# Delta rule: a substitution by rows for the 16x16 diagonal blocks of the inverses

## What is computed

```python
decay = jnp.exp(jnp.where(tri, g[..., :, None] - g[..., None, :], -jnp.inf))
kk = jnp.einsum("bnhcd,bnhsd->bnhcs", k, k)
lower = jnp.where(strict, beta[..., :, None] * kk * decay, 0.0)
rhs = jnp.concatenate([v * beta[..., None], k * (beta * jnp.exp(g))[..., None]], axis=-1)
sol = lax.linalg.triangular_solve(lower, rhs, left_side=True, lower=True, unit_diagonal=True)
```

## Time and profile before

| | before |
|---|---|
| median of 3 runs | 1775.28 us (1773.97 to 1776.09) |
| the profiled execution, its own time | 1773.64 us |
| span of the profile | 1771.5 us |
| granted TensorE clock, mean | 0.988 |
| TensorE matmul busy | 1679.3 us (95% of the span) |
| VectorE, ScalarE, GpSimd busy | 875.3, 783.6, 201.5 us |

### The profile page before, as it was taken

The page is one execution under the profiler, slowest core; times in us unless marked ns, Lnnn a source line. Parts: engine busy times, 40 slices in busy tenths (PEclk is TensorE's granted clock), DMA queues, the critical chain, the costliest instruction groups (busy, mean ns, idle before and its releaser), DMA issues.

```text
span 1771.5 us, 21811 instructions
## 1 busy us (share of the span) xinstructions
PE 1679.3 (95%) x8436; PEld 1334.6 (75%) x8436; DVE 875.3 (49%) x1388; ACT 783.6 (44%) x1345; POOL 201.5 (11%) x233
## 2 busy tenths in 40 slices
PE   6899999999988899999999799999997999999998
PEld 4678888888877687677777588777675888888867
DVE  4746556556554535455555543544336532344346
ACT  3533543543543424565665622555544432243243
POOL 0111211111102200023232300000002000000011
PEclk9899999999999999999999999999998999999999
DMA  4111111111110322322222122211121333233321
GB/s 167 60 36 36 60 48 37 60 49 36 60 37 24 111 96 84 114 78 72 78 70 69 36 96 95 68 50 58 48 72 48 107 100 100 90 103 101 102 72 48
DMA packets 40165, 127.29 MB, mean 72 GB/s; under 512 B 4576, under 2 KB 9104, under 8 KB 40064
## 3 DMA queue, kind: packets, MB, share of 16 engines
q1 hardware_dynamic: 38112, 121.65, 20.8%
q0 software_dynamic: 1040, 3.27, 0.5%
q10 hardware_dynamic: 912, 0.99, 0.2%
HBM read 122.69 MB, written 2.15 MB: 70 GB/s over the span
## 4 chain that ended last, share of the span: by engine, by line
PE 83%; DVE 7%; ACT 6%; issue 3%; POOL 1%; DMA 0%; SPq 0%; ACTq 0%; DVEq 0%
PE ps L637 81%; ACT L L1521 3%; DVE wl L1713 2%; DVE L L2162 1%; PE ps L975 1%; PE ps L783 1%; DVE qkv L1749 1%; POOL h L2409 1%; ACT wh L1126 1%; DVE qb L1800 0%; ACT L L1473 0%; DMA wraw<-in_wa 0%; DVE mo L2285 0%; ACT xr L1390 0%; DVE U L2026 0%
## 5 line engine op out<-in xcount | busy, mean ns | idle before, releaser
L637 PE MATMUL ps<-xr,wh 128*128 128x512 f32 x2752 | 906.9, 411 | 15.5 <-DVE wl L1713 14.1
L637 PEld LDWEIGHTS ps<-xr,wh 128*128 128x128 f32 x2752 | 502.7, 190 | 139.6 <-issue 36.5
L637 PE MATMUL ps<-xr,wl 128*128 128x512 f32 x1376 | 542.1, 394 | 0.0
L1713 DVE TENSOR_TENSOR wl<-wraw,wh 128x1024 fp32r<-128x1024 f32 x214 | 261.3, 1235 | 153.3 <-ACT wh L1126 151.8
L637 PEld LDWEIGHTS ps<-xr,wl 128*128 128x128 f32 x1376 | 260.4, 189 | 57.3
L1126 ACT ACTIVATE wh<-wraw 128x1024 fp32r<-128x1024 f32 x214 | 220.3, 1047 | 20.3 <-PE ps L637 17.8
L637 PE MATMUL ps<-xm,wh 128*128 128x512 f32 x640 | 200.8, 395 | 12.8 <-DVE xm L2278 8.6
L637 PEld LDWEIGHTS ps<-xm,wh 128*128 128x128 f32 x640 | 120.2, 189 | 44.2 <-issue 9.8
L637 PE MATMUL ps<-xm,wl 128*128 128x512 f32 x320 | 125.3, 392 | 0.0
L2394 POOL TENSOR_SCALAR L<-L,m 128x256 f32<-128x256 f32 (+1 forms) x128 | 75.6, 611 | 325.5 <-DVE m L2177 325.5
L2338 POOL TENSOR_TENSOR Mm<-AT,masks 128x512 f32<-128x512 f32 x56 | 82.8, 1485 | 239.3 <-PE ps L637 122.8
(11 more groups left out here) (240 smaller groups left out, 1946.5 us busy)
## 6 DMA issues: line engine op xcount, KB each, us to landing
wraw<-in_wa SPq DMA_DIRECT2D x48, 512.0 KB, 3.3
wraw<-in_wb SPq DMA_DIRECT2D x32, 512.0 KB, 3.3
wraw<-in_wu SPq DMA_DIRECT2D x32, 512.0 KB, 3.3
wraw<-in_wd SPq DMA_DIRECT2D x32, 512.0 KB, 3.3
wraw<-in_wao SPq DMA_DIRECT2D x16, 512.0 KB, 3.4
wraw<-in_wbo SPq DMA_DIRECT2D x16, 512.0 KB, 3.3
wraw<-in_wc SPq DMA_DIRECT2D x16, 512.0 KB, 3.3
bias<-rel_rows SPq DMA_DIRECT2D x16, 256.0 KB, 3.7
```

Source lines behind the costliest of these rows:

```text
L637: return e.matmul(out, w, x, start=start, stop=stop, skip_group_check=True)
L1713: e.tensor_tensor(m.wl[:, i % N_SPLIT, :], m.raw[:, i % N_RAW, :], m.wh[:, i % N_SPLIT, :].bitcast(F), ALU.subtract).then_inc(s.wlo, 1)
```

## The change

The four lowest levels (blocks up to 16x16) are no longer made by products. GpSimd masks A to the 16x16 diagonal blocks in one multiplication (`m16`, a mask summed once at the start). VectorE adds the blocks of a row up into a compact 128x64 tile `dc` (each partition holds the 16 entries of its block's row, for 4 chunks), and 15 shuffles, one for each row r, copy row r of each block to all 16 partitions of that block (`nb`). GpSimd starts from the unit matrix and, for each r, does a product and a sum on up to 4x15 elements of `uc`; each of the 31 instructions waits for the one before. VectorE spreads `uc` into `U` (`U3`) and transposes it in blocks of 32x32 (`T3`). Three levels of products remain (4, 5 and 6). The transposed factor is made from `U` each time: on VectorE for level 5, by TensorE for level 6. `prep` keeps its 28 steps; 16 calls on TensorE are left.

```diff
 # TensorE, prep: calls 8 to 15
-        o = begin(8)
-        e.wait_ge(s.prep_v, prep_v(h, "U0"))
-        end(8, turn4(o, lambda n: U[:, n, :]), (s.prep_a, prep_a(h, "T")))
-        yield
-        call = 9
-        for i in range(1, 7):
+        yield from idle(6)
+        call = 8
+        for i in range(4, 7):
...
-            if i < 6:
-                o = begin(call)
-                e.wait_ge(s.prep_a, prep_a(h, f"P{i}"))
-                e.wait_ge(s.prep_v, prep_v(h, f"U{i - 1}"))
-                end(call, four(o, lambda n: U[:, n, :], lambda n: m.Pm[:, n, :]), (s.prep_v, prep_v(h, f"T{i}")))
-                call += 1
...
+            if i == 5:
+                o = begin(call)
+                e.wait_ge(s.prep_v, prep_v(h, "U5"))
+                end(call, turn4(o, lambda n: U[:, n, :]), (s.prep_a, prep_a(h, "T5")))
+                call += 1
+                yield
 # VectorE, prep
+        e.wait_ge(s.prep_o, prep_o(h, "D"))
+        did(e.tensor_reduce(m.dc[:], m.Mm[:, 1].rearrange("p n (b c) -> p n c b", b=8), AX.X, ALU.add, negate=True))
         o = product(5)
...
-        e.wait_ge(s.prep_o, prep_o(h, "M0"))
-        did(e.tensor_tensor(U, m.ident.unsqueeze(1).to_broadcast([128, 4, 128]), m.Mm[:, 0], ALU.subtract))
-        yield
-        yield from idle(3)
+        yield
+        after("dc")
+        if h:
+            e.wait_ge(s.inv, N_INV * h)
+        for r in range(15):
+            e.stream_shuffle(m.nb[:, r], m.dc[:].rearrange("p n c -> p (n c)"), [r] * 16 + [16 + r] * 16).then_inc(s.rows16, 1)
+        yield
+        yield from idle(6)
+        e.wait_ge(s.inv, N_INV * (h + 1))
...
+        did(e.tensor_tensor(U.rearrange("p n (b c) -> p n b c", b=8), m.uc[:].unsqueeze(2).to_broadcast([128, 4, 8, 16]),
+                            m.m16.rearrange("p (b c) -> p b c", b=8).unsqueeze(1).to_broadcast([128, 4, 8, 16]),
+                            ALU.mult))
+        after("U3")
...
+        did(e.transpose(m.Tm[:].rearrange("p n c -> p (n c)"), U.rearrange("p n c -> p (n c)")))
+        yield
+        for call, i in ((9, 4), (11, 5), (14, 6)):
+            yield
             o = product(call)
             after(f"U{i - 1}")
             did(e.tensor_tensor(U, U, o, ALU.subtract))
+            if i == 4:
+                after("U4")
+                did(e.transpose(m.Tm[:].rearrange("p n c -> p (n c)"), U.rearrange("p n c -> p (n c)")))
 # GpSimd, new
+    def invert(h):
...
+        did(e.tensor_copy(m.uc[:], m.unit.unsqueeze(1).to_broadcast([128, 4, 16])))
+        done += 1
+        for r in range(15):
+            w = 15 - r
+            nb = m.nb[:, r].rearrange("p (n c) -> p n c", n=4)
+            part = m.bp.rearrange("p (n c) -> p n c", n=4)[:, :, 0:w]
+            e.wait_ge(s.rows16, 15 * h + r + 1)
+            e.wait_ge(s.inv, done)
+            did(e.tensor_tensor(part, nb[:, :, r + 1:], m.uc[:, :, r:r + 1].to_broadcast([128, 4, w]), ALU.mult))
+            e.wait_ge(s.inv, done + 1)
+            did(e.tensor_tensor(m.uc[:, :, r + 1:], m.uc[:, :, r + 1:], part, ALU.add))
+            done += 2
 # SyncE
-    def scale(to):
-        if to != "b":
-            split(pace.ahead(4))
```

More of the change, by code:

```diff
@@ L11 @@
 ALU = mybir.AluOpType
+AX = mybir.AxisListType
 KB = 1024
@@ L530, in __init__ @@
         self.rec_p, self.rec_a, self.rec_v = new("rec_pe"), new("rec_act"), new("rec_dve")
+        self.m16, self.unit, self.rows16, self.inv = (new(n) for n in ("block_mask", "block_unit", "block_rows", "block_inverse"))
         self.ohi, self.olo = new("o_hi"), new("o_lo")
@@ L1329, in prep @@
             yield
[L1330 to L1333, removed]
-        yield
-        call = 9
-        for i in range(1, 7):
+        yield from idle(6)
+        for call, i in ((8, 4), (10, 5), (13, 6)):
             o = product(call)[1]
-            if i > 1:
-                e.wait_ge(s.prep_p, prep_p(h, call - 1))
+            if i > 4:
+                e.wait_ge(s.prep_p, prep_p(h, 9 if i == 5 else 11))
             elif h:
-                e.wait_ge(s.prep_p, prep_p(h - 1, 25))
+                e.wait_ge(s.prep_p, prep_p(h - 1, 14))
             did(e.activation(m.Pm[:], o, ACT.Copy))
@@ L1344, in prep @@
             yield
-            call += 3 if i < 6 else 2
-        o = product(call)[1]
+            if i == 5:
+                o = product(12)[1]
+                e.wait_ge(s.prep_p, prep_p(h, 10))
+                did(e.activation(m.Tm[:], o, ACT.Copy))
+                yield
+        o = product(15)[1]
         if h >= 2:
@@ L2008, in prep @@
         did(e.tensor_tensor(m.kd[:, par], o, bc(m.ekd[:, col]), ALU.mult))
-        e.wait_ge(s.prep_o, prep_o(h, "M0"))
-        did(e.tensor_tensor(U, m.ident.unsqueeze(1).to_broadcast([128, 4, 128]), m.Mm[:, 0], ALU.subtract))
         yield
-        yield from idle(3)
-        call = 9
-        for i in range(1, 7):
-            yield
[L2016 to L2023, removed]
+        after("dc")
[4 more added lines that the diff above has]
+        yield
+        yield from idle(6)
+        e.wait_ge(s.inv, N_INV * (h + 1))
+        if h == 0:
+            e.wait_ge(s.m16, 4)
+        free_of_recurrence()
+        did(e.tensor_tensor(U.rearrange("p n (b c) -> p n b c", b=8), m.uc[:].unsqueeze(2).to_broadcast([128, 4, 8, 16]),
+                            m.m16.rearrange("p (b c) -> p b c", b=8).unsqueeze(1).to_broadcast([128, 4, 8, 16]),
+                            ALU.mult))
+        after("U3")
+        if h:
+            e.wait_ge(s.prep_p, prep_p(h - 1, 13))
+        did(e.transpose(m.Tm[:].rearrange("p n c -> p (n c)"), U.rearrange("p n c -> p (n c)")))
+        yield
+        for call, i in ((9, 4), (11, 5), (14, 6)):
+            yield
             o = product(call)
@@ L2330, in begin @@
         e.dma_start(m.masks[:], m.d["k_masks"]).then_inc(s.masks, 16)
+        e.wait_ge(s.masks, 16)
+        for n in range(1, 4):
+            if n > 1:
+                e.wait_ge(s.m16, n - 1)
+            e.tensor_tensor(m.m16, m.m16, m.masks[:, n, :], ALU.add).then_inc(s.m16, 1)
+        e.wait_ge(s.k1, 16)
+        e.wait_ge(s.m16, 3)
+        e.tensor_tensor(m.m16, m.m16, m.ident, ALU.add).then_inc(s.m16, 1)
+        t = m.masks[:, 1, :]
+        e.wait_ge(s.m16, 4)
+        e.tensor_tensor(t[:, 0:64], m.ident[:, 0:64], m.ident[:, 64:128], ALU.add).then_inc(s.unit, 1)
+        e.wait_ge(s.unit, 1)
+        e.tensor_tensor(t[:, 64:96], t[:, 0:32], t[:, 32:64], ALU.add).then_inc(s.unit, 1)
+        e.wait_ge(s.unit, 2)
+        e.tensor_tensor(m.unit, t[:, 64:80], t[:, 80:96], ALU.add).then_inc(s.unit, 1)
     @part
@@ L2335, in did, with level @@
             ins.then_inc(s.prep_o, 1)
-        def level(i):
-            did(e.tensor_tensor(m.Mm[:, i % 2], m.AT[:], m.masks[:, i, :].unsqueeze(1).to_broadcast([128, 4, 128]),
-                                ALU.mult))
+        def level(i, mask):
+            did(e.tensor_tensor(m.Mm[:, i % 2], m.AT[:], mask.unsqueeze(1).to_broadcast([128, 4, 128]), ALU.mult))
         yield
@@ L2346, in prep, with did @@
         if h == 0:
-            e.wait_ge(s.masks, 16)
+            e.wait_ge(s.m16, 4)
         else:
-            e.wait_ge(s.prep_p, prep_p(h - 1, 24))
+            e.wait_ge(s.prep_p, prep_p(h - 1, 10))
         e.wait_ge(s.prep_v, prep_v(h, "at"))
[L2351 to L2364, removed]
-        yield
+        level(1, m.m16)
+        yield
+        if h:
+            e.wait_ge(s.prep_p, prep_p(h - 1, 13))
+        level(4, m.masks[:, 4, :])
+        yield
+        yield
+        invert(h)
+        yield from idle(8)
+        e.wait_ge(s.prep_v, prep_v(h, "dc"))
+        level(5, m.masks[:, 5, :])
+        yield
+        e.wait_ge(s.prep_p, prep_p(h, 8))
+        level(6, m.masks[:, 6, :])
+        yield from idle(7)
+    def invert(h):
+        done = N_INV * h
+        def did(ins):
+            ins.then_inc(s.inv, 1)
+        if h:
+            e.wait_ge(s.prep_v, prep_v(h - 1, "U3"))
+        else:
+            e.wait_ge(s.unit, 3)
+        did(e.tensor_copy(m.uc[:], m.unit.unsqueeze(1).to_broadcast([128, 4, 16])))
[10 more added lines that the diff above has]
+            done += 2
     @part
```

26 lines of the change are left out of this document (14 added, 12 removed).

## The result

| | before | after |
|---|---|---|
| median of 20 runs | 1774.47 us (1772.51 to 1776.36) | 1777.49 us (1775.47 to 1778.97) |
| profiled span | 1771.5 us | 1777.2 us |
| granted clock, mean | 0.988 | 0.963 |

The ratio is 1.0016, 95% interval 1.001 to 1.0022. The forecast was 1762, a gain of 0.7%: the gain did not come. 1777.5 is inside the range given, far from its middle.

A forecast was written before the change was run, and what follows sets the result against it. TensorE, 95% busy, was taken as the bound. Six heads at 2.7 us (9.7 less stall, small waits and clock) gave -16, round 1 +3, round 8 -0.5: -13.5, so 1762 us; range 1738 to 1790, its own 1752 to 1771.

The forecast's parts named there:

- the mechanism: Rounds 2 to 7: TensorE loses 9.7 us of work a head, but then waits at P4 for VectorE's order behind ScalarE.
- GpSimd's chain: 30 dependent substitution instructions at 0.38 us, 11.4 us plus 2.5 of stretch; in round 4 hidden behind VectorE's order.
- The stall: TensorE idle ahead of P4 in rounds 2 to 7, 4.9 us a head, until VectorE has written U3 and T3.
- the clock: TensorE's clock falls behind the idle time ahead of P4: 1.2 us lost a head, also in rounds 1 and 8.
- the 13.7 that was summed: Time from P4 to `w` through the three remaining levels, 13.7 us, before the loss to the low clock.
- The ends: Rounds 1 and 8, where few or no projections hide the chain: 3 us lost in round 1, 0.5 gained in round 8.
- SyncE's removed part: Block loads on SyncE: removing this part costs nothing; otherwise a load comes a block late, 3 us once.
- C: Rival: GpSimd's chain is the bound, gain gone at 0.46 us an instruction, 1797 us at 0.55; chance 0.25 for over 0.2% slower.
- D: Rival: GpSimd's chain at 0.44 to 0.47 us an instruction, or a longer stall ahead of P4; within 0.2%, chance 0.13.
- A: The forecast itself: stall of 3.5 to 6 us a head set by VectorE's order behind ScalarE; 1752 to 1771 us, chance 0.46.
- B: Rival: larger cover, TensorE waits under 2.8 us and keeps its clock; 1738 us, or 1720 without stall; chance 0.16.
- The port rule: VectorE's port lock blocks GpSimd fully: stretch 3.3 us, not 2.5; still covered in round 4, round 1 0.8 us worse.

The follow-up runs named there:

- the single and the double removal: Against the changed kernel: U3 and T3 one iteration earlier on VectorE, 1769.4 us; GpSimd doing one of 15 substitution rows, 1765.3; both edits, 1730.4.
- dummies: Useless TensorE matmuls added to the changed kernel: five ahead of P4, 1766.0 us; only in rounds 1 and 8, ahead of P4 and each later call, 1766.7.

## Why the prediction was wrong

**Right: the mechanism and its place in the middle rounds.** On the axis of before, TensorE was ready for P4 at 282.2 (forecast 282.3), GpSimd's chain ended at 283.5 (284.4), the recurrence's pair started at 283.9 (284.0), and P4 at 287.3 (287.2). The stall is 5.05 us (4.9). A GpSimd step took 0.36 us (12.87 us for the 30, less the 2.2 of stretch given below; forecast 0.38), `dc` 1.04 us (0.4 to 1.2 were named as harmless), a shuffle 0.14 to the next (0.1 to 0.3). That U3 stood behind the pair, and that GpSimd was hidden behind it, were both as said; the single and the double removal show it.

**The step that failed: the clock.** The forecast gave it one price, 1.2 us a head, the same in the end rounds, read from one stretch of 3.8 us after an idle time. The sum so had 2.4 us for rounds 1 and 8, and nothing for round 2 beyond its own stall, or for the time behind the last `w`. The runs show two prices. In the middle rounds it is 1.6 us (15.79 against 14.20 with dummies), 0.4 over the forecast, and the chain without it is 14.2, 0.5 over the 13.7 that was summed: together nearly the whole distance from 2.7 to 1.73 us a head, 4.9 us over rounds 3 to 7. In rounds 1 and 8 it is another matter. In round 8 no projections follow P4, TensorE waits at each level, and its clock did not come back for the whole chain: 19.75 us from P4 to `w`, where the forecast had 13.7 + 1.2. In round 1 the clock came back, and fell again where the projections had run out: 16.29 us. The low clock then ran on, into round 2 (-2.7 became +0.5) and behind the last `w` (+2.7). The dummies in rounds 1 and 8 alone gave 10.8 us back.

**The ends otherwise.** P4 of round 1 was 1.5 us later than forecast (100.86 against 99.4), 1.3 of it from before the round's squares. P4 of round 8 was 0.8 us later, counted from the `w` before it. That the first of these comes so close is partly luck, since two errors cancel. Counted from the later start, GpSimd's chain ended 0.9 us earlier than forecast (98.26 against 97.9 + 1.3), and U3 took 1.0 us more:
```profile
98.29 1.72 DVE L2025 TENSOR_TENSOR U<-uc,masks 128x512 f32<-128x512 f32 x1 [6.23 <-POOL uc L2419]
```
GpSimd makes the next level's mask product (1.26 us from 98.20) right behind its last step, so it runs beside U3 just where U3 waits for GpSimd. Round 8 has the same, and so has the kernel with U3 earlier. No run here moves this product behind U3.

The +1.3 at the start is the clock in one group, as shown above. Why it fell there is open. The 24 matmuls took 7.3 us in all nine profiles with the mask additions at the start. Of the five without, four had 5.7 (the kernel before and three with later masks) and one had 7.3. So the additions may bring it about, though the median of the kernel with later masks shows no gain. The kernel before has times of both 1774.3 and 1776.3 us in one set, with mean clocks of 0.988 and 0.985 to 0.987; its profiled execution is one of the quicker. SyncE's removed part cost nothing that shows: from 6 us behind the last `w` on, the two profiles stay 5.2 to 5.7 us apart to the end.

**The sum.** Forecast -13.5, measured +5.7 in the spans: 19.2 us. Of it, 4.9 are rounds 3 to 7, 3.2 round 2, 1.7 round 1, 5.7 round 8, 2.7 behind it and 1.3 the start (rounded parts). By the medians only 3.0 were lost against before, so the distance is 16.5. The clock at the two ends is the largest part of it: 10.8 us by the dummies, of which 2.4 were in the forecast, so 8.4. Next are 5 us in the middle rounds, about equally clock and chain. Some 3 us are left, for the start and for U3 beside GpSimd; the medians can't part them.

**The rivals.** C had GpSimd's chain at over 0.46 us a step; it was 0.36. The time, 0.16% over before, falls in D's band (within 0.2%), but by neither of D's ways: the chain was not at 0.44 to 0.47, and the stall of 5.05 us is A's, not a longer one. So A's stall came with D's time, by a way that none of the rivals had. B, a cover large enough, needed both limits gone, as the 1730.4 us show. The port rule of the Trainium skill (SBUF — State Buffer) is taken up below.

## What to carry to other kernels

Work taken from an engine that is always busy is worth only what the next limits allow. Look for the second chain that ends close behind the first, since an edit that takes away one of them shows little: 8 and 12 us here, and 47 for both. The stall on TensorE was paid twice, once as the wait (5.05 us) and once as the clock behind it (1.6 us). In the bare chain of small dependent products of round 8 the second payment was 6.3 us, and 2.7 more behind it; price the rounds without filler apart from those with it. Moving one engine's part of a fixed order later was no cure as long as the other engines' parts of the same chain stood behind other work.

## What the runs showed of the hardware

- The clock fell behind an idle time of 5.05 us and was 0.50 for the 3.1 us that followed, in which TensorE was busy throughout:
```profile
291.97:295.10 3.13, 3.13 (x12) 2.80 (x12) 0.00 (x0) 0.60 (x1) 1.00 (x1) 0.50 0.00 0
```
In round 8, with TensorE busy 13.37 of 19.75 us, it did not rise at all; with dummies ahead of P4 and of 0.6 us between the calls it was 1.00 throughout. Behind an idle time of 2.02 us it was at the lower level for part of the 24 matmuls above in ten of fourteen profiles (7.3 us) and not in the other four (5.7 us).
- A GpSimd product of 24 elements took 1.26 us when VectorE's split of 1.22 us (282.50, two inputs in SBUF) ran beside it, 0.23 in round 8; the next block's input on VectorE (280.06, 0.69 us, one of its inputs in PSUM) did not touch the steps beside it:
```profile
280.00 0.26 POOL L2417 TENSOR_TENSOR masks<-xreg,uc 128x36 f32<-128x36 f32 x1
...
282.55 1.26 POOL L2417 TENSOR_TENSOR masks<-xreg,uc 128x24 f32<-128x24 f32 x1
283.89 0.59 POOL L2419 TENSOR_TENSOR uc<-uc,masks 128x24 f32<-128x24 f32 x1
```
It goes the other way too: U3 took 1.72 us beside GpSimd's product of 1.26 (rounds 1 and 8), 0.68 alone. By the Trainium skill (SBUF — State Buffer, section SBUF: two separate sides) the pair of ports that VectorE and GpSimd share is held for a whole instruction, and a VectorE instruction asks for it in a 2-port mode or with two inputs in SBUF. These rows agree, as far as they go: none shows a 2-port mode. In round 4 four steps were stretched by 2.2 us in all beside 3.5 us of such VectorE work; the forecast had 2.5. Two of the stretched steps can be matched: 282.41 is the end of one, 0.11 us behind a tap's, and 283.81 that of the next, 0.09 us behind the split's. The loss is less than 3.5 us because the four steps' own time runs within it: 3.5 less 4 x 0.36 is 2.1, an estimate.
- VectorE's small dependent instructions of 4 to 60 elements took 0.16 to 0.22 us, 0.26 to 0.29 from start to start in the mean of a pair; GpSimd's 0.21 to 0.32, and 0.36 in the mean. The fixed part is most of both: 60 elements take 0.29, four 0.21 us.
